# First late gate in pieces around the sample values, branch weights in another place, V pages from two queues

## The reference, cut to what matters

```python
def sb_block(q, k, v, q_pos, k_pos, bias):
    z = jnp.einsum('bqhd,bkhd->bhqk', q, k) * (HD_A ** -0.5) + bias[None, :, None, None]
    mask = k_pos[None, :] < q_pos[:, None]
    log_keep = jnp.where(mask, jax.nn.log_sigmoid(-z), 0.0)
    later = lax.cumsum(log_keep, axis=3, reverse=True) - log_keep
    w = jnp.where(mask, jnp.exp(jax.nn.log_sigmoid(z) + later), 0.0)
    return jnp.einsum('bhqk,bkhd->bqhd', w, v)
...
    k_past = cache_k[i][page_table].reshape(DB, -1, H_A, HD_A)     # 8 samples x 4 pages of 128 rows
    v_past = cache_v[i][page_table].reshape(DB, -1, H_A, HD_A)
...
    proj = jnp.einsum('blnc,ncd->blnd', branches, lp['w_branch'])
    gates = jax.nn.sigmoid(gl.reshape(B, L, N_BRANCH, D_MODEL))    # gl = h @ (part of w_in)
    x = x + jnp.sum(gates * proj, axis=2) @ lp['w_out']
```

## Time and profile before

| | |
|---|---|
| median of 3 runs | 2041.4 us (2040.62 to 2041.47) |
| the profiled execution | 2046.39 us, its span 2044.7 us |
| mean granted TensorE clock | 0.974 |
| TensorE busy | 1925.9 us, 94% |
| VectorE, ScalarE, GpSimd busy | 993.4, 555.8, 385.9 us |
| mean DMA rate | 62 GB/s |

### The profile page before, as it was taken

The page is one execution under the profiler, slowest core; times in us unless marked ns, Lnnn a source line. Parts: engine busy times, 40 slices in busy tenths (PEclk is TensorE's granted clock), DMA queues, the critical chain, the costliest instruction groups (busy, mean ns, idle before and its releaser), DMA issues.

```text
span 2044.7 us, 28358 instructions
## 1 busy us (share of the span) xinstructions
PE 1925.9 (94%) x11697; PEld 1795.4 (88%) x11697; DVE 993.4 (49%) x1162; ACT 555.8 (27%) x749; POOL 385.9 (19%) x200
## 2 busy tenths in 40 slices
PE   8999898898895999999999999999999999998998
PEld 5889797884684889898899999999999999998898
DVE  6912563823371121212143566657666766766622
ACT  4223413214362111101233322122221221231710
POOL 1332222220110011011111212112211211121221
PEclk9999898998998999999989999999999999999999
DMA  5312211132204212021121111101110110110121
GB/s 186 45 53 74 71 60 56 58 136 94 64 22 153 88 52 73 31 73 41 45 91 63 63 52 62 41 21 62 51 41 31 62 41 21 62 51 31 61 74 42
DMA packets 52538, 127.59 MB, mean 62 GB/s; under 512 B 12626, under 2 KB 28530, under 8 KB 50162
## 3 DMA queue, kind: packets, MB, share of 16 engines
q1 hardware_dynamic: 40370, 98.91, 14.3%
q0 software_dynamic: 5184, 19.01, 3.0%
q10 hardware_dynamic: 6912, 8.65, 1.2%
HBM read 107.58 MB, written 19.06 MB: 62 GB/s over the span
## 4 chain that ended last, share of the span: by engine, by line
PE 84%; DVE 6%; issue 4%; ACT 3%; DMA 1%; SPq 1%; POOL 1%; ACTq 0%; DVEq 0%; POOLq 0%
PE ps L648 52%; PE ps L635 7%; PE ps L616 7%; PE ps L1029 6%; PE pst L1029 2%; PE ps L793 2%; DVE H L1902 1%; PE ps L714 1%; PE ps L864 1%; PE ps L894 1%; PE pst L883 1%; DVE H L1891 1%; ACT H L1448 1%; PE ps L622 1%; DVE BIG L1875 1%
## 5 line engine op out<-in xcount | busy, mean ns | idle before, releaser
L1998 POOL TENSOR_TENSOR Ul<-BIG,Uh 128x1024 fp32r<-128x1024 f32 x60 | 144.6, 2409 | 745.6 <-ACT Uh L1395 692.2
L648 PE MATMUL ps<-Nh,Uh 128*128 128x352 f32 x1248 | 270.5, 325 | 2.8 <-DVE H L1891 1.4
L648 PE MATMUL ps<-Nh,Ul 128*128 128x352 f32 x1248 | 269.0, 323 | 0.0
L648 PE MATMUL ps<-Fl,Uh 128*128 128x352 f32 x1248 | 268.8, 324 | 0.0
L648 PE MATMUL ps<-Hh,Uh 128*128 128x352 f32 x960 | 215.2, 333 | 15.7 <-DVE BIG L1830 5.8
L648 PEld LDWEIGHTS ps<-Nh,Uh 128*128 128x128 f32 x1248 | 212.6, 189 | 3.8 <-issue 3.5
L648 PEld LDWEIGHTS ps<-Nh,Ul 128*128 128x128 f32 x1248 | 214.3, 188 | 0.0
L648 PEld LDWEIGHTS ps<-Fl,Uh 128*128 128x128 f32 x1248 | 211.9, 188 | 0.0
L648 PE MATMUL ps<-Hh,Ul 128*128 128x352 f32 x960 | 208.4, 325 | 0.0
L648 PEld LDWEIGHTS ps<-Hh,Uh 128*128 128x128 f32 x960 | 165.1, 191 | 24.5 <-issue 7.8
L1830 DVE TENSOR_TENSOR BIG<-BIG,ps 128x1056 f32<-128x1056 f32 x32 | 40.1, 1254 | 274.9 <-PE ps L616 272.3
(11 more groups left out here) (283 smaller groups left out, 3037.1 us busy)
## 6 DMA issues: line engine op xcount, KB each, us to landing
BIG<-in_wu SPq DMA_DIRECT2D x44, 512.0 KB, 3.6
H<-in_wd SPq DMA_DIRECT2D x11, 1024.0 KB, 4.9
BIG<-in_wgl SPq DMA_DIRECT2D x20, 512.0 KB, 4.3
BIG<-in_x SPq DMA_DIRECT2D x16, 528.0 KB, 6.0
gates<-BIG ACTq DMA_DIRECT2D x48, 176.0 KB, 1.9
BIG<-in_wz POOLq DMA_DIRECT2D x16, 512.0 KB, 3.8
BIG<-gates SPq DMA_DIRECT2D x6, 1056.0 KB, 8.4
BIG<-in_wge POOLq DMA_DIRECT2D x12, 512.0 KB, 3.8
```

Of the source, the lines that this page charges most:

```text
L648: ins = nc.tensor.matmul(psb(3 * out + g), w[wp][:, k], x[xp][k][:, t0:t0 + n], start=(k == 0 and wp == xp), stop=(k == kk - 1 and wp == 1))
L1998: nc.gpsimd.tensor_tensor(Ul[:, half], uraw[:, half], Uh[:, half].bitcast(F32), ALU.subtract)\
```

## The change

- The region takes `mwb` before `early` and `SIG`, so it lies over the attention's `KB` and `wT2`, and no longer over page buffers.
- `m_slot(i, u)`: in round 0 units 0 to 3 all use slot 0. The first late gate (unit 3 of round 0) is accumulated in slot 1, chunk by chunk, by `gate_piece`: chunks 0 to 4 before `sample_values(range(4, 8))`, chunk 5 after it, chunk 6 after the transposes, chunk 7 after the projection of unit 0. Units 1 to 3 wait for the multiply of the unit before.
- Of the 16 page loads that were left at the end of SyncE's list, groups 14 and 15 (8 loads) go to GpSimd's queue with a semaphore of their own. SyncE loads the first two late weights before groups 12 and 13.
- GpSimd rounds and splits the first two late weights itself (`first_late`), one before and one after its page loads; ScalarE no longer does.
- The first branch weights wait for `a_pv` >= 16 (all prompt values), not for the last page; early gate 0 and the second branch weights stand ahead of `page_used` >= 16, the other early gates and branch C's rows behind it.

```diff
+        mwb = r.take(2, 4, 2, P)
         early = r.take(EARLY, T)
         SIG = r.take(2, T)
-        mwb = r.take(2, 4, 2, P)
...
+        def m_slot(i, u):
+            return 0 if isinstance(i, int) and i == 0 and u <= EARLY else u % 2 if u < EARLY else 1
...
-            for n in range(4, 2 * DB):
+            for n in range(4, 2 * DB - 4):
                 sp.wait_ge(S("page_used"), n - 3)
                 page_in(n)
...
             for v in range(2):
                 sp.wait_ge(S("w_lo"), ZB + FILLS - 1 + v)
                 late_weights(0, v)
+            for n in range(2 * DB - 4, 2 * DB - 2):
+                sp.wait_ge(S("page_used"), n - 3)
+                page_in(n)
             sp.wait_ge(S("stored"), outs)
             sp.wait_ge(S("a_sc"), 32)
             sp.wait_ge(S("as_sc"), 1)
             sp.dma_start(Z[:, XD:XD + 2, :], spill[0]).then_inc(S("d_rows"), 16)
-            sp.wait_ge(S("page_used"), 2 * DB)
-            sp.dma_start(Z[:, GC:GC + 2, :], spill[1]).then_inc(S("c_rows"), 16)
+            sp.wait_ge(S("a_pv"), 16)
             branch_weights(0, 0)
-            branch_weights(0, 1)
-            sp.wait_ge(S("a_over"), 2)
             for s in range(2):
                 sp.wait_ge(S(f"gate_stored{s}"), 16 * 3 * FILLS // 2)
-            early_gates(0)
+            early_gate(0, 0)
+            branch_weights(0, 1)
+            sp.wait_ge(S("page_used"), 2 * DB)
+            early_gate(0, 1)
+            sp.dma_start(Z[:, GC:GC + 2, :], spill[1]).then_inc(S("c_rows"), 16)
...
+            def gate_piece(ks):
+                for k in ks:
+                    for w, x in ((Uh, Hh), (Uh, Hl), (Ul, Hh)):
+                        for g, (t0, n) in enumerate(SPANS):
+                            ins = nc.tensor.matmul(psb(3 + g), w[:, 0, k], x[:, k, t0:t0 + n],
+                                                   start=(k == 0 and w is Uh and x is Hh),
+                                                   stop=(k == KD - 1 and w is Ul))
+                return ins
+            pe.wait_ge(S("gate_out"), 3 * FILLS)
+            pe.wait_ge(S("w_lo"), MLO + 1)
+            gate_piece(range(5))
             sample_values(range(4, 8))
-            ins = None
             pe.wait_ge(S("page_used"), 16)
             pe.sem_inc(S("as_pv"), 1)
+            gate_piece((5,))
             pe.wait_ge(S("as_out"), 3)
...
             ins.then_inc(S("as_pv"), 1)
+            gate_piece((6,))
             pe.wait_ge(S("a_over"), 2)
...
+                    first = isinstance(i, int)
+                    if first and 1 <= u <= EARLY:
+                        pe.wait_ge(S("m_pfree"), u)
+                    elif u >= EARLY:
...
+                        if first and v == 1:
+                            pe.wait_ge(S("m_pfree"), u)
                         dense3(0, (Uh[:, v % 2], Ul[:, v % 2]), (chunks(Hh), chunks(Hl)), KD).then_inc(S("m_gate"), 1)
...
+                    if first and u == 0:
+                        gate_piece((KD - 1,)).then_inc(S("m_gate"), 1)
...
-            act.wait_ge(S("gate_done"), 3 * FILLS)
-            for v in range(2):
-                late_high(0, v)
             act.wait_ge(S("a_over"), 2)
...
+            def first_late(v):
+                pool.wait_ge(S(f"uw_in{v}"), 32)
+                pool.wait_ge(S("gate_done"), 3 * (FILLS - 1 + v))
+                nc.gpsimd.tensor_copy(Uh[:, v], uraw[:, v]).then_inc(S("w_hi"), 1)
+                pool.wait_ge(S("w_hi"), SPLITS + v + 1)
+                nc.gpsimd.tensor_tensor(Ul[:, v], uraw[:, v], Uh[:, v].bitcast(F32), ALU.subtract)\
+                    .then_inc(S("w_lo"), 1)
...
+            first_late(0)
+            for n in range(2 * DB - 2, 2 * DB):
+                pool.wait_ge(S("page_used"), n - 3)
+                bb = PV_ORDER[n - DB]
+                for g in range(PAGES):
+                    page = pool.value_load(pt[0:1, bb * PAGES + g:bb * PAGES + g + 1], min_val=0, max_val=39)
+                    pool.dma_start(vp[n % 4][:, g], a["cv"][ds(page, 1)].rearrange("o p c -> (o p) c"))\
+                        .then_inc(S("late_pages"), 16)
+            first_late(1)
```

More of the change, by code:

```diff
@@ L395, in spans @@
                     x.rearrange("p (g t) -> p g t", g=3))
-        def m_slot(u):
-            return u % 2 if u < EARLY else 1
+        def m_slot(i, u):
+            return 0 if isinstance(i, int) and i == 0 and u <= EARLY else u % 2 if u < EARLY else 1
         block = ctx.enter_context(nc.Block())
@@ L501, in _, with early_gate @@
             out("k_cm", Z[:, KA:KA + 2, :])
-            for n in range(4, 2 * DB):
+            for n in range(4, 2 * DB - 4):
                 sp.wait_ge(S("page_used"), n - 3)
                 page_in(n)
[L507 to L510, removed]
+            def early_gate(i, g):
+                n, m = ((0, 1), (1, EARLY - 1))[g]
+                sp.dma_start(early[:, n:n + m], gates[ds(i * EARLY + n + QKS, m)].rearrange("n p t -> p n t"))\
+                    .then_inc(S(f"early_in{g}"), 16)
             def late_weights(i, v):
@@ L543, in _ @@
                 sp.wait_ge(S("m_sig"), i * 8 + (EARLY - 8))
-                early_gates(i)
+                early_gate(i, 0)
+                early_gate(i, 1)
                 for v in range(2):
@@ L913, in sample_values @@
                         j, e = divmod(bb, 2)
-                        if g == 0:
+                        if g == 0 and v < 6:
                             pe.wait_ge(S(f"pages_in{v % 4}"), 16 * PAGES * (v // 4 + 3))
+                        elif g == 0:
+                            pe.wait_ge(S("late_pages"), 16 * PAGES * 2)
                         ins = nc.tensor.matmul(ps[0][32 * j:32 * j + 32, e * HW:e * HW + HW],
@@ L967, in m_round @@
                         pe.wait_ge(S("mb_in"), i * 16 + 16)
-                    if u >= EARLY:
+                    first = isinstance(i, int)
+                    if first and 1 <= u <= EARLY:
+                        pe.wait_ge(S("m_pfree"), u)
+                    elif u >= EARLY:
                         v = u - EARLY
@@ L979, in m_round @@
                         wait_prior(pe, S("m_pfree"), i * 8 + (u - 1))
-                    if u >= EARLY or u == 1:
+                    if (u >= EARLY or u == 1) and not (first and u <= EARLY):
                         wait_prior(pe, S("m_pfree"), i * 8 + (u if u > 1 else 0))
@@ L985, in m_round @@
                         pe.wait_ge(S("d_rows"), 32)
-                    dense(m_slot(u), mwb[:, q, n], Z[:, BRANCH_AT[n]:BRANCH_AT[n] + 2, :], 2)\
+                    dense(m_slot(i, u), mwb[:, q, n], Z[:, BRANCH_AT[n]:BRANCH_AT[n] + 2, :], 2)\
                         .then_inc(S("m_proj"), 1)
+                    if first and u == 0:
+                        gate_piece((KD - 1,)).then_inc(S("m_gate"), 1)
             rounds(pe, 4, m_round)
@@ L1377, in m_round @@
                         act.wait_ge(S("m_added"), i * 8 + (u - 1))
-                    nc.scalar.activation(spans(SIG[:, u % 2]), spans(early[:, u]) if u < EARLY else slab(0), ACT.Sigmoid)\
+                    nc.scalar.activation(spans(SIG[:, u % 2]), spans(early[:, u]) if u < EARLY else
+                                         slab(int(isinstance(i, int) and i == 0 and u == EARLY)), ACT.Sigmoid)\
                         .then_inc(S("m_sig"), 1)
@@ L1829, in m_round @@
                         sig = SIG[:, u % 2]
-                        v.tensor_tensor(spans(ACC if n == 0 else sig), spans(sig), slab(m_slot(u)), ALU.mult)\
+                        v.tensor_tensor(spans(ACC if n == 0 else sig), spans(sig), slab(m_slot(i, u)), ALU.mult)\
                             .then_inc(S("m_pfree"), 1)
@@ L1982, in _ @@
                 split(r_)
+            def first_late(v):
[5 more added lines that the diff above has]
+                    .then_inc(S("w_lo"), 1)
             def late_low(n, v):
-                pool.wait_ge(S("late_hi"), n)
+                pool.wait_ge(S("late_hi"), n - 2)
                 nc.gpsimd.tensor_tensor(Ul[:, v % 2], uraw[:, v % 2], Uh[:, v % 2].bitcast(F32), ALU.subtract)\
                     .then_inc(S("w_lo"), 1)
+            first_late(0)
[7 more added lines that the diff above has]
+            first_late(1)
             def late_round(i):
-                for v in range(LATE):
+                for v in range(2 if isinstance(i, int) else 0, LATE):
                     late_low(i * LATE + (v + 1), v)
@@ L1996, in tile_low @@
             def tile_low(r, half):
-                pool.wait_ge(S("late_hi"), r * 2 + (4 * LATE + half + 1))
+                pool.wait_ge(S("late_hi"), r * 2 + (4 * LATE + half - 1))
                 nc.gpsimd.tensor_tensor(Ul[:, half], uraw[:, half], Uh[:, half].bitcast(F32), ALU.subtract)\
```

## The result

| | before | after |
|---|---|---|
| median of the runs | 2041.43 us (2040.62 to 2045.25) | 2029.09 us (2024.78 to 2029.99) |
| profiled execution, span | 2044.7 us | 2023.2 us |
| TensorE busy | 1925.9 us | 1912.8 us |
| mean granted TensorE clock | 0.974 | 0.984 |

The ratio is 0.9932, with a 95% interval of 0.9913 to 0.9951: 10 to 18 us faster, where I had forecast 20.9. In a second round of runs the same two kernels gave 2026.76 and 2042.15, ratio 0.9926 (0.9914 to 0.9939). The median of 2029.09 lies 0.09 us above the top of my range, that of the second round inside it.

What follows compares the result with a forecast made beforehand. TensorE bounds the kernel (84% of the span), idling for V pages, then branch weights, between attention and the first merge round. Unit 4's gate starts 20.9 us earlier: 2046.4 to 2025.5, less 5.0 to the median, 2020.5; range 2016 to 2029.

Steps and rivals of the forecast that it cites:

- Part 1, issue rate: Last V pages, half on GpSimd's queue: 1.4 us a page, bounds 1.33 and 2.2, last issued at about 643.0.
- Part 1, landing: GpSimd's last V page: lands 2.1 us after issue, plus 1.4 for SyncE's loads beside it, at 646.5.
- part 3: Branch weights ahead of the first merge round: issued early, there by 649.4, 3 us before unit 0 starts at 652.5.
- rival (a): Last V pages: GpSimd issues slowly, 2.2 us a page, last lands at 654.2, time 2028 us; chance 0.17.
- (c): Last V pages: transfers set the landing, at 651.6 as before, 5.1 us later than counted, 2025.6 us; chance 0.05.
- Rival (b): TensorE's page wait: the clock falls, second sample values take 4.1 instead of 1.9 us; + 4.6, 2025 us; chance 0.14.
- Part 2: First late gate in pieces: five pieces, 7.3 us, run under the page wait; chain from values to result loses 0.8 us.
- Part 4: Units 0 to 3 through one PSUM slot: 20.4 us instead of 30.0 to unit 4's gate, with three waits of 1.54.
- The sum: Start of unit 4's gate: 672.9 instead of 693.79, 20.9 us less, whole time 2020.5 us.

Runs made afterwards that it cites:

- the hold: Kernel after, with SyncE issuing the spilled rows of D, branch weights and early gate 0 only when GpSimd's pages have landed; median 2020.53 us, ratio 0.9895.
- experiment 2: Kernel after, with all 16 last page loads on SyncE's queue again and the rest kept; median 2029.6 us.

## Why the prediction was right or wrong

**Part 1, issue rate: right in kind, too cautious.** GpSimd issued a page every 1.16 us, but for one early step of 1.46:

```profile
635.27 0.54 POOL L2031 DMA_DIRECT2D BIG<-in_cv  x1 [0.62 <-issue]
636.43 0.54 POOL L2031 DMA_DIRECT2D BIG<-in_cv  x1 [0.62 <-issue]
```

My 1.4 was high, and 1.16 lies under my lower bound of 1.33, because I had added the DMA instruction to SyncE's step as if nothing overlapped; in the chain a table read at 635.25 (0.29 us) lies beside the DMA instruction of 635.27. The last issue was 6.3 us after E, where I had 7.1.

**Part 1, landing: the step that failed.** I had counted 2.1 us to the landing and added 1.4; it took 6.9. I had priced the traffic that my own part 3 puts beside the pages at 1.4 us and it cost about 4.2 (6.9 against 2.7 with the hold). The page came 13.2 us after E, not 10.6: 2.6 us. This is neither rival (a) nor (c) as I told them; transfers delay the landing, but because of the neighbour, not because of the page rate. What the Trainium skill says against the part ("DMA: Bandwidth & Descriptors", section "Issuing engines are not separate DMA queues"), that DMAs of several issuers interleave on the same DMA engines, fits what mattered; that the issue time saved is usually small doesn't hold here (3 to 4 us by experiment 2).

**Rival (b), the clock, came true beside it.** The values took 3.7 us, not 1.9, and piece 5 took 2.05, not 1.46: 2.3 us together. I gave it 0.14, on a wait of 3.3 us; the wait was 0.6 and then 4.1 us.

**Part 2.** The five pieces ran from E without a gap, and the weights' split fell together with one slow multiply on VectorE (1.74 us instead of 1.09) that reached no chain: from the end of the fill that allows the split to E it is 34.7 us in both kernels. Undoing parts 2 and 4 cost 6.8 to 7.6 us; the sum in the prediction makes it 8.8 (9.6 in part 4 less 0.8 in part 2), the expectation before the run 7.6 (50 against 42.4).

**Part 3.** No DMA released a projection, and rows of C were in time. But the early issue isn't free: its cover holds and its side effect on the pages costs.

**Part 4.** 21.1 us against 20.4: the three waits took 1.4 to 1.5 us each between the busy stretches as expected, but a projection that nothing follows ends 3.82 us after its start; I had used 3.55, the distance to the next matmul in a full queue.

**The sum.** Stage 42.4 against 36.9, 5.5 us short: 2.6 landing, 2.3 clock, 0.7 part 4 (rounded). The whole time missed by 8.6; I put the other 3.1 down to the spread between runs, which is not shown: in the second round the medians differ by 15.4 us, where the stage gained 57.8 - 41.6 = 16.2, with D of before from its one profile. Taking the profiled execution of before, 5.0 above its median, as the base of the sum did no harm; taking one median as sharp to a microsecond did. And there is luck in how near the range came: its top was set by slow issues on GpSimd, rival (a), which didn't happen (1.16 us a page, not 2.2); a late landing together with the slow clock brought the time to the same place.

## What to carry to other kernels

When loads are moved to a second queue, look at what the first queue sends next: a large load issued beside the last small ones of the other delayed them by 2 to 4 us here, and holding it until they had landed gave more (5 to 6 us of the stage) than the second queue itself (3 to 4). A wait on the critical engine costs its own length and often the slow clock after it (in after 4.1 us of wait, then 2.3 us more for the values and piece 5), so count both. When whole times spread by several us, compare one stage between two marks in each trace, and repeat a profile before a small gain in it is believed.

## What was not expected of the hardware

- Beside up to about 1 MB of another queue's loads, the landing of a 128 KB load grows (2.7, 4.95, 6.9 us at 0, 0.5 and 1.1 MB), beyond that no growth shows (6.0 to 7.2 us at 1.6 to 2.7 MB). Whether the size or the lead of those loads decides isn't separated.
- The same kernel with the same waits of a few us was at full clock in one execution and well under it in another (granted clock 1.00 or 0.66 around the values; values 1.92 or 3.21 us, first projection 3.82 or 5.30), 4 us of stage D, of which 1.2 us came from the landing.
- GpSimd issues a page load with an address read from a table every 1.16 us, about as fast as SyncE's 1.10 to 1.24.
